# A fused transformer kernel on one core: x and mem also loaded turned, the small vectors as one array, and the first loads in another order

## The chip, the cores and the metric

The kernel runs on one core of a Trainium2 chip. The metric is the device time of one execution in microseconds (us); lower is better. A profiled execution is recorded separately; its trace gives the rows below, in us from the first instruction.

## The reference

Two transformer blocks stand one behind the other on x of 256 tokens by 1024 channels; mem holds another 256 rows of 1024. All is float32. The part that matters here is the first layer of the first block:

```
mem_n = rmsnorm(mem, norm_mem)
h = rmsnorm(x, norm_mix[0])
mkv = mem_n @ w_mem_kv[0]                  # 1024 x 512: keys and values of the memory
q, k, v, qm = split(h @ w_in_a[0])         # 1024 x 1536
y = concat(windowed_gqa(q, k, v, sink_a), memory_attn(qm, mk, mv))
x = x + y @ w_out[0]
x = x + (silu(gate) * up) @ w_down[0]      # h = rmsnorm(x, norm_ffn[0]); gate, up = h @ w_gate_up[0]
```

The second layer, with neighbourhood attention, and the second block (sparse attention, a recurrence, a convolved feed-forward layer) follow. rmsnorm divides each token by the root of its mean square and multiplies each channel by a gain. The kernel applies the gain per channel before the product and the root per token after it.

## The kernel before, in words

Every product is cut into parts. A part is a piece of a weight matrix of up to 1 MB (4 times 128 rows by 512 columns) that SP loads into one of four buffers raw0 to raw3. ACT rounds it to a high half (hi, the line with `split` in the ACT program) and DVE subtracts to get a low half (lo); there are three buffers of each. PE then makes three matmuls per 128 rows and per half of the tokens: high by high, low by high, high by low. The activations need the same two halves with the channels in the partitions: memTh, memTl for mem, xTh, xTl for x. SP may load into a raw buffer again as soon as the low half of the piece four before is made (`lo_made`). Parts 0 to 3 are the first product with mem (pieces of 0.26, 0.26, 0.52 and 1.05 MB), parts 4 and 5 the first tile of h @ w_in_a, parts 6 and 7 the second.

A class `Order` writes one list of steps; each engine's program goes through that list and emits what is its own in each step, so the list sets the order on ACT, DVE, POOL and PE alike. Steps that can wait go into a queue `later`, from which some are taken between parts and between the two chunks of twelve matmuls of a 1 MB part.

At the start SP loads mem (with the tokens in the partitions), four weight pieces, the small vectors in sixteen small loads, x, and then the weights. ACT's queue loads the identity and norm_mem, POOL's the constants of the scores. PE turns mem in four steps `memx` of two blocks of 128 channels each (four 128 by 128 transposes by the identity), x in four steps `xin`, and the vectors in one step `rows`; ACT writes the high and DVE the low half from the PSUM bank, each scaled with the gain of the channel. Step `memsq` squares and sums mem on ACT, DVE makes the mean, POOL the root; steps `sq` do the same for x, a half of the channels each.

When the mem tile is done, its evacuation stores one half in `mstage` on ACT and one on DVE, and in step `mk` PE turns mstage; mstage lies in the tensor `early`. Both the evacuation and `mk` need the root of mem. Lines: the transposes 833 and 835, the matmuls 855 to 857, the squares 1040, the evacuation 1087 and 1092, the high halves of weights 1175, of mem 1183 and of x 1195, the low halves 1600, 1624 and 1640, the root 1814, SP's loads from 1956 on.

Of the kernel before, what the change touches and what calls it, by code (L numbers as in the profile page):

```python
# [131 lines left out]
class Order:  # L132
# [53 lines left out]
    def put(self, *task):  # L186
        kind = task[0]
        if kind in ("memgain", "rows", "rel", "columns"):
            self.turn(task, ON_D)
            self.made.add(kind)  # L190
        elif kind == "memx":
            self.turn(task, ON_D)
# [4 lines left out]
        elif kind == "xin":  # L197
            self.turn(task, ON_D)
# [357 lines left out]
def build(nc, a, out):  # L556
    ctx = ExitStack()
    with ctx:
# [11 lines left out]
        d_mem, d_norm, d_x, d_rows, d_ident, d_const = (sem(n) for n in ("d_mem", "d_norm", "d_x", "d_rows", "d_ident", "d_const"))  # L570
# [42 lines left out]
        cols = sb("cols", [128, 128 + 96 + 88])  # L613
        small = sb("small", [128, 184])
# [15 lines left out]
        sink = small[:, 16:28]  # L630
        steep = small[:, 10:16]
# [4 lines left out]
        memgain = small[:, 144:152]  # L636
        m8 = small[:, 160:176]
# [16 lines left out]
        rows = early[:, 2048:2432].rearrange("p (n d) -> p n d", n=3)  # L654
        memx = early[:, 0:2048].rearrange("p (t d) -> p t d", t=2)
        memrow = early[0:8, 2432:2560]
# [36 lines left out]
        rel = small[0:32, 152:160]  # L693
# [55 lines left out]
        def ready(source, k):  # L749

            if source == "mem":
                return emptied(("memx", k // 2 * 2))
# [6 lines left out]
            what, l = source  # L759
            if what == "in":  # L760
                return emptied(("xin", l, k // 2 * 2))
# [62 lines left out]
        def tensor_program(e):  # L824
# [91 lines left out]
            for step in order.steps:  # L916
# [3 lines left out]
                elif kind == "memgain":  # L920
                    e.wait_ge(d_norm, 16)
                    e.wait_ge(d_ident, 16)
                    e.transpose(claim(step)[:, 0:8], memrow, ident[0:8, 0:8]).then_inc(x_full, 1)
                elif kind == "memx":
                    e.wait_ge(d_mem, 16)
                    turned(claim(step), blocks_of(memx, name[0] * 128, 2))
                elif kind == "rows":
                    e.wait_ge(d_rows, 256)
                    bank = claim(step)
                    e.transpose(bank[:, 0:128], rows[0:128, 0, :], ident)  # L930
                    e.transpose(bank[:, 128:224], rows[0:96, 1, :], ident[0:96, 0:96])
                    e.transpose(bank[:, 224:312], rows[0:88, 2, :], ident[0:88, 0:88]).then_inc(x_full, 1)
                elif kind == "xin":
                    s, k = name
                    if s == 0:
                        e.wait_ge(d_x, 16)
                    else:
                        e.wait_ge(acc_dve, order.res_at[s, k // 4])
                    turned(claim(step), blocks_of(xres, k * 128, 2))
                elif kind == "mk":  # L940
                    t_ = order.tile_of["mem", name[0], 0]
# [92 lines left out]
        def scalar_program(e):  # L1034
# [8 lines left out]
            def attention(stage, i):  # L1043
# [15 lines left out]
                if 0 <= i - 1 < n:  # L1059
# [6 lines left out]
                    else:  # L1066
                        e.wait_ge(max_made, 4 * stage + i)
                        src = x_bank(("S", stage, i - 1))[:, :].rearrange("p (t k) -> p t k", t=2)
                        if i - 1 >= len(s_slots[stage]):
                            e.wait_ge(x_full, filled(("P", stage, i - 1 - len(s_slots[stage]))))  # L1070
                        elif stage == 0:
                            e.wait_ge(x_full, filled(("memx", 6)))
# [94 lines left out]
            for step in order.steps:  # L1167
# [10 lines left out]
                elif kind == "memx":  # L1178
                    k = name[0]
                    e.wait_ge(x_full, filled(step))  # L1180
                    e.wait_ge(*emptied(("memgain",)))
                    for j in range(2):
                        e.activation(memTh[:, k + j, :], x_bank(step)[:, j * 256:(j + 1) * 256], ACT.Copy, scale=memgain[:, k + j:k + j + 1]).then_inc(x_high, 1)
                elif kind == "memsq":
                    e.wait_ge(d_mem, 16)
                    for j in range(2):
                        for t in range(2):
                            square(0, j, t, memx[:, t, j * 512:(j + 1) * 512])
                elif kind == "xin":
                    s, k = name  # L1190
                    gain = col((0, 2, 1, 3)[s])
                    e.wait_ge(x_full, filled(step))
                    e.wait_ge(*emptied(("rows",)))
                    for j in range(2):
                        e.activation(xTh[:, k + j, :], x_bank(step)[:, j * 256:(j + 1) * 256], ACT.Copy, scale=gain[:, k + j:k + j + 1]).then_inc(x_high, 1)
# [14 lines left out]
                elif kind == "pair":  # L1210
# [3 lines left out]
                    if l == 0 and what == "q" and at < 6:  # L1214
                        e.wait_ge(d_const, 32)
# [141 lines left out]
        def vector_program(e):  # L1357
# [50 lines left out]
            def soften(stage, i):  # L1408
# [10 lines left out]
                else:  # L1419
                    if i >= len(s_slots[stage]):  # L1420
                        e.wait_ge(x_full, filled(("P", stage, i - len(s_slots[stage]))))
                    if stage == 0:
                        e.wait_ge(d_const, 32)
# [170 lines left out]
            for step in order.steps:  # L1594
# [20 lines left out]
                elif kind == "memgain":  # L1615
                    e.wait_ge(x_full, filled(step))
                    e.tensor_copy(memgain, x_bank(step)[:, 0:8]).then_inc(x_dve, 1)
                elif kind == "memx":
                    k = name[0]
                    if k == 0:  # L1620
                        e.wait_ge(*emptied(("memgain",)))
                    e.wait_ge(x_high, order.high_at[step])
                    for j in range(2):
                        done = e.scalar_tensor_tensor(out=memTl[:, k + j, :], in0=x_bank(step)[:, j * 256:(j + 1) * 256], scalar=memgain[:, k + j:k + j + 1],
                                                      in1=memTh[:, k + j, :].bitcast(F), op0=ALU.mult, op1=ALU.subtract)
                    done.then_inc(x_dve, 1)
# [434 lines left out]
```

## Time and profile before

| what | us |
|---|---|
| median of 3 runs | 1112.36 |
| lowest and highest run | 1109.60, 1112.61 |
| the profiled execution | 1111.92 |
| its span, first to last instruction | 1110.1 |
| PE busy | 1041.9 (94%) |
| DVE busy | 738.4 (67%) |
| ACT busy | 587.1 (53%) |
| POOL busy | 116.8 (11%) |

The profiled execution's own time is 1.8 us longer than its span. The mean granted clock of PE is 0.975 of full speed. Busy shares are means over the whole span.

### The profile page before, as it was taken

The page shows a single profiled execution, that of the slowest core. Times are in us where ns is not written, and L with a number is a line of the kernel's source. Part 1 is how long each engine was busy: PE and PEld are TensorE (multiplying, and loading weights), DVE is VectorE, ACT ScalarE, POOL GpSimd, SP SyncE. Part 2 cuts the span into 40 slices and gives each one's busy share as a digit, 9 for nine tenths or more (in the row PEclk, how much of TensorE's full clock was granted, in tenths as well). Part 3 has the DMA queues.
Part 4 walks back from the last instruction along what each step waited for, and adds up shares of the span by engine and source line. Part 5 has one row for each costly group of instructions (what it writes and reads, how often), then busy time and mean ns, then how long its engine had stood idle before and what let it go on. Part 6 is the DMA issues. An engine that isn't in the chain of part 4 may idle for free.

```text
span 1110.1 us, 13563 instructions
## 1 busy us (share of the span) xinstructions
PE 1041.9 (94%) x5224; PEld 864.3 (78%) x5224; DVE 738.4 (67%) x984; ACT 587.1 (53%) x834; POOL 116.8 (11%) x159
## 2 busy tenths in 40 slices
PE   5997996999999999899999999998989989999996
PEld 5876875888888777788888888787767778888885
DVE  4667773465455567578888656669867766777753
ACT  6547562444345557544443445467656456666631
POOL 1013130000000013110000011012551000000001
PEclk9998998999999999999999979999999989999999
DMA  9655378655556441379999784435463535465441
GB/s 335 227 141 71 113 206 211 203 195 182 176 172 208 152 153 39 114 258 366 335 337 328 296 264 151 159 121 172 160 199 114 190 133 190 154 193 184 157 147 38
DMA packets 97825, 209.28 MB, mean 189 GB/s; under 512 B 5650, under 2 KB 13282, under 8 KB 94626
## 3 DMA queue, kind: packets, MB, share of 16 engines
q1 hardware_dynamic: 93313, 194.46, 52.0%
q0 software_dynamic: 4288, 13.89, 5.6%
q8 instruction: 42, 0.69, 0.3%
q14 instruction: 22, 0.17, 0.0%
q10 hardware_dynamic: 160, 0.07, 0.0%
HBM read 205.25 MB, written 4.57 MB: 189 GB/s over the span
## 4 chain that ended last, share of the span: by engine, by line
PE 73%; DVE 9%; ACT 7%; issue 4%; DMA 4%; POOL 2%; SPq 1%; ACTq 0%; DVEq 0%; POOLq 0%
PE bank L855 21%; PE bank L857 21%; PE bank L856 21%; PE bank L833 4%; ACT hi L1175 3%; DVE lo L1600 3%; DMA big<-scratch_rpb 2%; PE bank L869 2%; PE bank L835 1%; POOL big L1885 1%; PE bank L969 1%; DMA raw<-in_w_down 1%; DVE xres L1475 1%; DMA small<-in_sink_a 1%; DMA scratch_rpb<-in_rpb_b 1%
## 5 line engine op out<-in xcount | busy, mean ns | idle before, releaser
L1600 DVE TENSOR_TENSOR lo<-raw,hi 128x2048 fp32r<-128x2048 f32 (+1 forms) x164 | 367.4, 2242 | 219.1 <-ACT hi L1175 218.4
L1175 ACT ACTIVATE hi<-raw 128x2048 fp32r<-128x2048 f32 (+1 forms) x164 | 303.5, 1852 | 203.7 <-PE bank L857 156.9
L855 PE MATMUL bank<-hi,xTh 128*128 128x512 f32 (+2 forms) x896 | 346.9, 387 | 10.4 <-DVE lo L1600 10.4
L857 PE MATMUL bank<-hi,xTl 128*128 128x512 f32 (+2 forms) x896 | 337.7, 377 | 0.0
L856 PE MATMUL bank<-lo,xTh 128*128 128x512 f32 (+2 forms) x896 | 337.6, 377 | 0.0
L855 PEld LDWEIGHTS bank<-hi,xTh 128*128 128x128 f32 x896 | 170.3, 190 | 42.2 <-DVE lo L1600 11.0
L857 PEld LDWEIGHTS bank<-hi,xTl 128*128 128x128 f32 x896 | 170.0, 190 | 31.7
L856 PEld LDWEIGHTS bank<-lo,xTh 128*128 128x128 f32 x896 | 170.6, 190 | 28.6 <-issue 0.2
L855 PE MATMUL bank<-hi,hTh 128*128 128x512 f32 x264 | 103.5, 392 | 0.5 <-DVE lo L1600 0.5
L857 PE MATMUL bank<-hi,hTl 128*128 128x512 f32 x264 | 102.8, 389 | 0.0
L856 PE MATMUL bank<-lo,hTh 128*128 128x512 f32 x264 | 102.8, 389 | 0.0
L1814 POOL TENSOR_TENSOR rms<-rms,small 128x2 f32<-128x2 f32 x9 | 6.4, 715 | 510.3 <-DVE rms L1368 326.6
L855 PEld LDWEIGHTS bank<-hi,hTh 128*128 128x128 f32 x264 | 49.6, 188 | 11.0 <-DVE lo L1600 0.9
L857 PEld LDWEIGHTS bank<-hi,hTl 128*128 128x128 f32 x264 | 49.5, 188 | 10.4
L856 PEld LDWEIGHTS bank<-lo,hTh 128*128 128x128 f32 x264 | 49.6, 188 | 10.0
L1612 DVE SCALAR_TENSOR_TENSOR big<-raw,small,big 128x2048 f32<-128x2048 f32 x24 | 56.3, 2345 | 0.0
L1590 DVE SCALAR_TENSOR_TENSOR big<-bank,cols,big 128x255 f32<-128x255 f32 (+2 forms) x100 | 41.2, 475 | 8.7 <-ACT big L1339 7.7
L833 PE MATMUL bank<-const,nrm 128*128 128x128 f32 x201 | 35.8, 290 | 6.1 <-DVE nrm L1702 5.3
L1040 ACT ACTIVATE junk<-xres 128x512 bf16<-128x512 f32 x32 | 20.2, 632 | 37.0 <-DVE xres L1533 27.3
L833 PEld LDWEIGHTS bank<-const,nrm 128*128 128x128 f32 x201 | 27.6, 151 | 13.4 <-DVE nrm L1702 5.8
L1160 ACT ACTIVATE hTh<-bank 128x512 fp32r<-128x512 f32 x22 | 13.2, 598 | 33.1 <-PE bank L835 33.0
L1339 ACT ACTIVATE big<-bank,cols 128x256 f32<-128x256 f32 x44 | 22.4, 559 | 13.9 <-PE bank L835 13.9
(348 smaller groups left out, 1358.5 us busy)
## 6 DMA issues: line engine op xcount, KB each, us to landing
raw<-in_w_gate_up SPq DMA_DIRECT2D x44, 1024.0 KB, 5.4
raw<-in_w_down SPq DMA_DIRECT2D x30, 1024.0 KB, 5.1
raw<-in_w_ada SPq DMA_DIRECT2D x24, 1024.0 KB, 6.4
raw<-in_w_up SPq DMA_DIRECT2D x22, 1024.0 KB, 5.1
raw<-in_w_in SPq DMA_DIRECT2D x21, 1024.0 KB, 5.1
raw<-in_w_out SPq DMA_DIRECT2D x12, 1024.0 KB, 5.0
raw<-in_w_in_b SPq DMA_DIRECT2D x10, 1024.0 KB, 5.1
raw<-in_w_in_a SPq DMA_DIRECT2D x6, 1024.0 KB, 10.0
```

What stands on the lines that cost most here:

```text
L833: e.transpose(bank[:, i * 128:(i + 1) * 128], x, ident)
L855: e.matmul(o, sh, h[:, k, :], start=p.first and k == 0, stop=False)
L856: e.matmul(o, sh, lo[:, k, :], start=False, stop=False)
L857: done = e.matmul(o, sl, h[:, k, :], start=False, stop=p.last and k == p.nk - 1)
L869: done = e.matmul(bank[:, n * 256:(n + 1) * 256], q[x][:, n * 128:(n + 1) * 128], k[y], start=x + y == 0, stop=x == 1)
L1040: e.activation(junk[:, :], x, ACT.Square, accum_out=rms[i][:, 2 * j + t:2 * j + t + 1]).then_inc(squared, 1)
L1160: e.activation(o, view, ACT.Copy).then_inc(x_high, 1)
L1175: e.activation(hi_s[m % SPLITS][:, 0:n], raw[p.at % RAWS][:, 0:n], ACT.Copy).then_inc(hi_made, 1)
L1339: e.activation(cv[:, j, :], x_bank(task)[:, j * 256:(j + 1) * 256], ACT.Identity, bias=CVB(kt + j), scale=CVW(2, kt + j)).then_inc(conv_be ...
L1590: e.scalar_tensor_tensor(out=o[:, j, n:], in0=bank[:, j * 256:j * 256 + 256 - n], scalar=weights[j][n - 1], in1=o[:, j, n:], op0=ALU.mult, ...
L1600: e.tensor_tensor(lo_s[s][:, 0:n], raw[p.at % RAWS][:, 0:n], hi_s[s][:, 0:n].bitcast(F), ALU.subtract).then_inc(lo_made, 1)
L1612: e.scalar_tensor_tensor(out=piece, in0=raw[i % RAWS][:, :], scalar=small[:, k:k + 1], in1=piece, op0=ALU.mult, op1=ALU.add).then_inc(ada_ ...
```

## The change

x and mem are also given turned, with the channels in the partitions (`xT`, `memT`), and are loaded so into nrm and early. PE no longer turns them or the vectors, which arrive in one array of 128 by 330 on ACT's queue. mem in its first form goes into xres, for its squares alone; x comes into xres afterwards, on POOL's queue behind the root of mem, and the constants of the scores follow it there. The list has the steps of the start in another order.

```diff
         elif kind == "memx":
-            self.turn(task, ON_D)
             self.made |= {("mem", task[1]), ("mem", task[1] + 1)}
...
         elif kind == "xin":
-            self.turn(task, ON_D)
+            if task[1]:
+                self.turn(task, ON_D)
...
     def run(self):
-        self.put("memgain")
         for k in range(0, 8, 2):
+            self.put("memx", k)
             self.split_through(min(k // 2, SPLITS - 1))
-            self.put("memx", k)
-        self.later.append(("memsq",))
-        self.later.append(("rows",))
-        self.later.append(("relload",))
-        for j in range(2):
-            self.pieces(0, j)
+        self.later.extend([("rows",), ("xin", 0, 0), ("xin", 0, 2), ("memsq",), ("xin", 0, 4), ("xin", 0, 6), ("relload",), ("sq", 0, 0), ("sq", 0, 1)])
...
-        memx = early[:, 0:2048].rearrange("p (t d) -> p t d", t=2)
+        memT = early[:, 0:2048].rearrange("p (k t) -> p k t", k=8)
+        xT = nrm[:, :, :].rearrange("p t (k n) -> p (t k) n", k=4)
...
+            e.dma_start(cols[:, :], a["vectors"]).then_inc(d_vec, 16)
             e.dma_start(ident, a["constants"][:, 0:128]).then_inc(d_ident, 16)
-            e.dma_start(memrow, a["norm_mem"].rearrange("(k p) -> k p", p=128)).then_inc(d_norm, 16)
...
                 elif kind == "memx":
                     k = name[0]
-                    e.wait_ge(x_full, filled(step))
-                    e.wait_ge(*emptied(("memgain",)))
+                    if k == 0:
+                        e.wait_ge(d_vec, 16)
+                    e.wait_ge(d_memT[min(k // 2, 2)], 16)
...
                 elif kind == "memsq":
                     e.wait_ge(d_mem, 16)
                     for j in range(2):
                         for t in range(2):
-                            square(0, j, t, memx[:, t, j * 512:(j + 1) * 512])
+                            square(0, j, t, xres[:, t, j * 512:(j + 1) * 512])
...
-            e.dma_start(const[:, 128:1408], a["constants"][:, 128:1408]).then_inc(d_const, 16)
-            e.dma_start(steep, a["constants"][:, 1408:1414]).then_inc(d_const, 16)
...
                 if kind == "memsq":
                     e.wait_ge(pool_const, 2)
                     root(0, 1)
+                    e.dma_start(xres[:, :, :], a["x"][0].rearrange("(t p) d -> p t d", p=128)).then_inc(d_x, 16)
+                    e.dma_start(const[:, 128:1408], a["constants"][:, 128:1408]).then_inc(d_const, 16)
...
-            e.dma_start(memx, a["mem"][0].rearrange("(t p) d -> p t d", p=128)).then_inc(d_mem, 16)
-            for i in range(RAWS):
-                load(i)
...
+            e.dma_start(memT[:, 0:2, :], a["memT"][:, 0:2, :]).then_inc(d_memT[0], 16)
+            next_load(0)
+            next_load(1)
+            e.dma_start(memT[:, 2:4, :], a["memT"][:, 2:4, :]).then_inc(d_memT[1], 16)
+            next_load(2)
+            e.dma_start(memT[:, 4:8, :], a["memT"][:, 4:8, :]).then_inc(d_memT[2], 16)
+            next_load(3)
+            e.dma_start(xT[:, 0:4, :], a["xT"][:, 0:4, :]).then_inc(d_xT[0], 16)
+            next_load(4)
+            e.dma_start(xres[:, :, :], a["mem"][0].rearrange("(t p) d -> p t d", p=128)).then_inc(d_mem, 16)
+            e.dma_start(xT[:, 4:8, :], a["xT"][:, 4:8, :]).then_inc(d_xT[1], 16)
+            for i in range(5, len(plan)):
+                next_load(i)
```

`next_load` is the load of one weight piece with its wait for the low half of the piece four before.

The orders at the three places of which the prediction speaks, as the two programs have them. First ACT from its first step on; before, up to the second raw0 (memTh and xTh are high halves of mem and x, junk the discarded output of a square):

```order
L1175 ACT_TABLE_LOAD
L1175 ACTIVATE hi<-raw 128x512 [waits d_raw0]
...
L1040 ACTIVATE junk,rms<-early 128x512 [waits d_mem]
L1040 ACTIVATE junk,rms<-early 128x512 [waits squared] x3
L1175 ACTIVATE hi<-raw 128x2048 [waits part_done,d_raw3]
L1195 ACTIVATE xTh<-bank,cols 128x256 [waits x_dve,x_full]
L1195 ACTIVATE xTh<-bank,cols 128x256
L1175 ACTIVATE hi<-raw 128x2048 [waits part_done,d_raw0]
```

With the change, down to the evacuation of the mem tile (the last row):

```order
L1165 ACT_TABLE_LOAD [waits d_memT0]
L1165 ACTIVATE memTh<-early,cols 128x256 [waits d_vec]
...
L1180 ACTIVATE xTh<-nrm,cols 128x256 [waits d_xT0]
L1180 ACTIVATE xTh<-nrm,cols 128x256
L1156 ACTIVATE hi<-raw 128x2048 [waits part_done,d_raw3]
...
L1021 ACTIVATE junk,rms<-xres 128x512 [waits d_mem]
L1021 ACTIVATE junk,rms<-xres 128x512 [waits squared] x3
L1156 ACTIVATE hi<-raw 128x2048 [waits part_done,d_raw0]
...
L1021 ACTIVATE junk,rms<-xres 128x512 [waits squared,d_x]
L1021 ACTIVATE junk,rms<-xres 128x512 [waits squared]
L1068 ACTIVATE early<-bank,rms 128x256 [waits acc_first,root_made]
```

The table load has taken over a wait; two blocks of x have moved ahead of the high half of raw3, and the squares of mem from before that half to before the one of the second raw0. The squares of x stood ahead of the evacuation before too; the load for which they wait has moved. POOL with the change, from its memsets to the load of x:

```order
L1819 MEMSET ones 128x128
L1791 ISA
L1791 TENSOR_TENSOR rms<-rms,small 128x2 [waits mean_made,pool_const]
L1825 DMA xres<-in_x 128x2x1024
L1826 DMA const<-in_constants 128x1280
```

Before, the constants were POOL's first load, and x was loaded by SP ahead of w_in_a. PE with the change, at the end of the first chunk of part 4 (the rows on early are the turn of mstage, step `mk`):

```order
L851 MATMUL bank<-hi,xTh 128x512 [waits in_low]
L852 MATMUL bank<-lo,xTh 128x512
L853 MATMUL bank<-hi,xTl 128x512
L829 MATMUL bank<-const,early 128x128 [waits acc_dve,acc_act,d_ident]
L829 MATMUL bank<-const,early 128x128 x2
L831 MATMUL bank<-const,early 128x128
```

This turn has not moved; it stood between the same two chunks before. Beyond part 5 all five orders are the same but for bank numbers and one wait less here and there.

## Rows read from the trace of the kernel before

**Rows 1.** The page: busy times and the chain that ended last.

```profile
PE 1041.9 (94%) x5224; PEld 864.3 (78%) x5224; DVE 738.4 (67%) x984; ACT 587.1 (53%) x834; POOL 116.8 (11%) x159
...
PE 73%; DVE 9%; ACT 7%; issue 4%; DMA 4%; POOL 2%; SPq 1%; ACTq 0%; DVEq 0%; POOLq 0%
```

**Rows 2.** Waits of PE, 0 to 30: us in total, times, longest.

```profile
PE bank L930 <- DMA small<-in_sink_a: 4.0, 1, 4.0
PE bank L855 <- DVE memTl L1624: 1.2, 1, 1.2
```

**Rows 3.** The chain that ended last, 0 to 120: start, us, what.

```profile
9.15 7.19 DMA small<-in_sink_a
...
22.87 0.33 PE bank L833 x3
...
94.54 0.48 DVE early L1432
```

**Rows 4.** Windows: PE, PEld, DVE, ACT, POOL busy, PEclk, DMA share, GB/s.

```profile
1.00:2.00 1.00, 0.00 (x0) 0.00 (x0) 0.00 (x0) 0.17 (x1) 0.76 (x2) 1.00 0.16 8
2.00:3.00 1.00, 0.00 (x0) 0.00 (x0) 0.00 (x0) 1.00 (x1) 0.79 (x3) 1.00 0.58 131
...
10.00:11.00 1.00, 0.25 (x1) 0.28 (x2) 1.00 (x3) 1.00 (x4) 0.00 (x0) 1.00 1.04 383
...
13.00:14.00 1.00, 0.00 (x0) 0.00 (x0) 1.00 (x4) 0.97 (x4) 0.00 (x0) 1.00 1.19 192
...
16.00:17.00 1.00, 0.61 (x4) 0.61 (x4) 0.33 (x2) 1.00 (x3) 0.31 (x1) 0.50 1.03 399
```

**Rows 5.** Timeline of PE: start, us, engine, line, what.

```profile
17.46 0.63 PE L856 MATMUL bank<-lo,memTh 128*128 128x512 f32 x1
17.89 0.63 PE L857 MATMUL bank<-hi,memTl 128*128 128x512 f32 x1
...
29.55 0.39 PE L855 MATMUL bank<-hi,xTh 128*128 128x512 f32 x1
...
32.28 0.49 PE L833 MATMUL bank<-const,early 128*128 128x128 f32 x3
```

**Rows 6.** Timeline of ACT: its table load.

```profile
1.83 1.28 ACT L1175 ACT_TABLE_LOAD   x1 [1.83 <-issue]
```

**Rows 7.** Timelines of ACT, DVE and POOL: squares, halves, root, evacuation.

```profile
13.11 0.68 ACT L1040 ACTIVATE junk<-early 128x512 bf16<-128x512 f32 x1
...
16.04 1.89 ACT L1175 ACTIVATE hi<-raw 128x2048 fp32r<-128x2048 f32 x1
...
17.47 0.57 POOL L1875 DMA_DIRECT2D small<-in_rel_bias  x1
...
17.97 2.29 DVE L1600 TENSOR_TENSOR lo<-raw,hi 128x2048 fp32r<-128x2048 f32 x1 [0.20 <-ACT hi L1175]
...
20.15 0.84 ACT L1195 ACTIVATE xTh<-bank,cols 128x256 fp32r<-128x256 f32 x2 [2.21 <-PE bank L835]
...
24.07 0.63 ACT L1040 ACTIVATE junk<-xres 128x512 bf16<-128x512 f32 x1
...
25.45 1.90 ACT L1175 ACTIVATE hi<-raw 128x2048 fp32r<-128x2048 f32 x1
...
28.68 0.49 ACT L1087 ACTIVATE early<-bank,rms 128x256 f32<-128x256 f32 x1
```

**Rows 8.** DMA issues: KB each, us from issue to landing.

```profile
early<-in_mem SPq DMA_DIRECT2D x1, 1024.0 KB, 5.4
const<-in_constants POOLq DMA_DIRECT2D x1, 640.0 KB, 7.2
small<-in_rel_bias POOLq DMA_DIRECT2D x1, 1.0 KB, 5.3
gbc<-in_norm_final POOLq DMA_DIRECT2D x1, 512.0 KB, 7.9
```

**Rows 9.** Queues in windows 6:7 (two), 21:22, 479:480: packets, MB, share.

```profile
q0 software_dynamic: 61, 0.31, 74.7%
q1 hardware_dynamic: 60, 0.12, 30.6%
...
q0 software_dynamic: 35, 0.02, 7.5%
...
q0 software_dynamic: 45, 0.18, 44.6%
```

More of the change, by code:

```diff
@@ L187, in put @@
         kind = task[0]
-        if kind in ("memgain", "rows", "rel", "columns"):
+        if kind in ("rel", "columns"):
             self.turn(task, ON_D)
@@ L629, in build @@
         half_ = small[:, 8:10]
-        sink = small[:, 16:28]
-        steep = small[:, 10:16]
+        sink, steep = cols[:, 312:324], cols[:, 324:330]
         negsink = small[:, 80:92]
@@ L759, in ready @@
             what, l = source
+            if what == "in" and l == 0:
+                return in_low, k // 2 + 1
             if what == "in":
@@ L919, in tensor_program @@
                     matmuls(parts[name[0]], name[1])
[L920 to L933, printed above, removed]
+                elif kind == "xin" and name[0]:
                     s, k = name
[L935 to L938, printed above, removed]
+                    e.wait_ge(acc_dve, order.res_at[s, k // 4])
                     turned(claim(step), blocks_of(xres, k * 128, 2))
                 elif kind == "mk":
+                    e.wait_ge(d_ident, 16)
                     t_ = order.tile_of["mem", name[0], 0]
@@ L1973, in sync_program, with next_load @@
-            e.dma_start(sink, bass.AP(a["sink_a"].tensor, 0, [[0, 128], [1, 12]])).then_inc(d_rows, 16)
-            e.dma_start(xres[:, :, :], a["x"][0].rearrange("(t p) d -> p t d", p=128)).then_inc(d_x, 16)
             weight_no = {i: m for m, i in enumerate(order.weights)}
-            for i in range(RAWS, len(plan)):
-                if plan[i - RAWS][0] == "ada":
+            def next_load(i):
+                if i >= RAWS and plan[i - RAWS][0] == "ada":
                     e.wait_ge(ada_done, order.ada_at[i - RAWS])
-                else:
+                elif i >= RAWS:
@@ L2015, in shape_constants @@
     key = np.arange(256)
[L2016 removed]
+    c = np.zeros((128, 1408), np.float32)
     c[:, 0:128] = np.eye(128)
@@ L2028, in shape_constants, with vectors_of, turned_blocks @@
     return c
+def vectors_of(a):
+    rows = [a[n].reshape(-1, 128) for n in ("norm_mix", "norm_ffn", "norm_mem", "g_mix_2", "g_ffn_2", "c_2", "conv_rnn_w_2", "conv_rnn_b_2",
+                                            "b_rg_2", "b_ig_2", "lru_lambda_2")]
+    taps = a["conv_ffn_w_2"].reshape(-1, 128)
+    rows += [taps[0:88], a["b_in_2"][0, 2376:3400].reshape(-1, 128), taps[88:132], a["conv_ffn_b_2"].reshape(-1, 128)]
+    steep = [[0.125 * 2.0 ** (8.0 * (2 * k + (i >= 64) + 1) / 12) for k in range(6)] for i in range(128)]
+    sink = np.broadcast_to(a["sink_a"].reshape(1, 12), (128, 12))
+    return np.ascontiguousarray(np.concatenate([np.concatenate(rows).T, sink, steep], axis=1).astype(np.float32))
+def turned_blocks(x):
+    return np.ascontiguousarray(x[0].T.reshape(8, 128, 256).transpose(1, 0, 2))
 def distance_buckets():
@@ L2050 @@
     given["constants"] = shape_constants()
+    given["vectors"] = vectors_of(given)
+    given["xT"], given["memT"] = turned_blocks(given["x"]), turned_blocks(given["mem"])
     given["onehot"] = distance_buckets()
+    for name in ("norm_mix", "norm_ffn", "norm_mem", "g_mix_2", "g_ffn_2", "c_2", "conv_rnn_w_2", "conv_rnn_b_2", "b_rg_2", "b_ig_2", "lru_lambda_2",
+                 "conv_ffn_w_2", "conv_ffn_b_2", "sink_a"):
+        del given[name]
     for name, v in given.items():
```

71 lines of the change are left out of this document (24 added, 47 removed).

## The prediction

> **What bounds the kernel now.** I read the page first. TensorE (PE) is busy for 94% of the span and the chain that ended last lies on it for 73% [rows 1]; a DMA holds 4% of that chain. So time is won or lost only where PE stands idle or runs at the low clock, and this change touches only the first 40 us. Next I read PE's waits in that stretch: after its first matmuls it stands for 4.0 us until the sink vector lands [rows 2]. The chain explains it: sixteen small loads are issued by SP one by one behind the first four weight pieces, and the last of them, issued at 9.15, lands at 16.34 [rows 3]. From 16.39 to 35.5 PE never waits. The windows show that the transfers are saturated all that time: about 383 to 399 GB/s, with a dip to 192 while the small loads run [rows 4]. PE's clock is 0.50 after the wait: matmuls start 0.43 us apart at 17.46 and 17.89, where later twelve of them take 2.73 us, 0.23 each [rows 4, 5]. The mark I measure against is PE at 29.55, when it starts part 4 (the first piece of w_in_a), and at 32.28, when after twelve matmuls it turns mstage, the stored half of the mem tile [rows 5].
>
> **The change: bytes and landings.** The vectors come as one array; x and mem are loaded twice, once turned, so 2.1 MB are added to a saturated stretch. SP's order is now memT 0.26, raw0 0.26, raw1 0.26, memT 0.26, raw2 0.52, memT 0.52, raw3 1.05, xT 0.52, raw0 again 1.05, mem 1.05, xT 0.52, raw1 again 1.05 (MB), with 0.24 MB on ACT's queue. By 3.0 us 0.14 MB had moved, and then 0.395 MB per us [rows 4]. This gives xT's first half at 12.5, the second raw0 at 15.2, **mem at 17.9**, xT's second half at 19.2, the second raw1 at 21.8. The same sum for raw3 before comes out some 0.7 us too early, which I keep as its error. SP waits for the first low half before the second raw0; that is made by about 8 us while the queue still has work until 12.5, so this costs nothing.
>
> **PE's starts.** Eight turns of four transposes and the turn of the vectors leave PE. One such turn holds PE for 0.33 us [rows 3], so with the vectors' about 2 us of PE work after 16.39 go; they count only if PE is then the last to be ready. It isn't. ACT's table load of 1.28 us [rows 6] now stands behind the landing of the first memT piece, so the first high half begins near 5.5; parts 0 to 2 then run between about 8 and 15, hidden from the end. Part 3 needs raw3's high and low halves. ACT waits for xT at 12.5, converts two blocks (0.84), then 1.9 for the high half and 2.25 until the low half is usable [rows 7]: part 3 starts near 17.5 and ends at 23.0 warm, 24.4 with cold matmuls, before the next thing is ready in either case. Part 4's split stands in ACT's order behind the four squares of mem, now read from xres, and those wait for mem: 17.9, plus 2.93 for the squares, 1.9 and 2.3 for the two halves, gives 25.1 against 29.55. Up to here the change is **4.4 us ahead**.
>
> **The new wait.** The load of x has moved from SP at 9.56 to POOL, behind the root of mem's mean, because it overwrites mem in xres. From the first square to the issue behind the root it is 4.36 us before (13.11 to 17.47) [rows 7]; so x is issued at 22.3. In ACT's order two squares of x stand ahead of the evacuation of the mem tile; PE's turn of mstage waits for that evacuation and stands between the twelve and twelve matmuls of part 4, so all of PE is queued behind it. PE wants the turn at 25.1 + 2.73 = 27.8. It gets it at the landing of x, plus 1.38 for two squares (24.07 to 25.45), 0.5 for the evacuation [rows 7], 0.05 to be seen: landing + 1.95.
>
> When does x land? No row shows a 1 MB load on POOL's queue in a saturated stretch. Below: mem itself, 1 MB on SP's queue with constants beside it, took 5.4 us [rows 8], which gives 27.7. Above: norm_final took 7.9 us for 512 KB on POOL's queue [rows 8], twice that gives 38; but its 128 readers want one and the same row. Nearer is the 640 KB of constants on the same queue beside SP's weights. It is POOL's first load, issued by 2 us, and lands at 8.4; from 6 to 7 it moved 61 packets to SP's 60, and 0.31 of 0.43 MB, since its packets are 5 KB and SP's 2 KB [rows 9]. rel_bias, 1 KB, issued at 17.47 in full traffic, took 5.3 us, and its queue first shows packets after 21 [rows 8, 9]. So I take 4.0 us until x begins, then packet for packet 4 KB of x to 2 KB of weights, two thirds of 0.395, 3.9 us, and 0.1: **x lands at 30.3**. The bounds kept for the range are 27.7 and, at norm_final's 0.18 MB per us [rows 9] behind 4.5 us, 33.2. The Trainium skill (DMA: Bandwidth & Descriptors, section on queues, rings and completion order) says that each DMA engine goes round the queues packet by packet; by that rule the trace agrees where it counts 61 to 60. The section on the anatomy of one DMA fits a transfer from GpSimd as 2.0 us plus bytes by 436 GB/s; for x that is an estimate of 4.4 us in place of 8.0. The constants' 7.2 us for 640 KB speaks against it here.
>
> PE then goes on at 30.3 + 1.95 = 32.25, against 32.28 before: the 4.4 us are gone. It has stood for 4.4 us. Before, 4.0 us of idleness were followed by three windows at clock 0.50, 1.2 GHz [rows 2, 4]; seven matmuls at 0.43 in place of 0.23 are 1.4 us.
>
> **Everything behind it.** Part 5 needs raw1's low half at 29.0, and part 6, whose split stands behind the evacuation, is ready some 5 us after the turn and wanted 8.6 after it. The constants for the scores now follow x and land near 33, first used at 94.54 [rows 3]. The later order of all engines is the same but for bank numbers, and PE fills that stretch, so the shift is carried to the end. **Sum: 32.25 - 32.28 + 1.4 = +1.4 us** on the profiled execution's 1111.92, so 1113.3; the median of the runs stands 0.44 above that execution, so I say 1113.7, within 0.3% (3.3 us), about what a measurement here can tell from no change.
>
> **Rivals.** In general the shift is landing of x - 28.9 us if PE cools down, and 1.4 less if it doesn't.
> *x crawls (slower).* If x moves at norm_final's rate behind a start as late as that of rel_bias, it lands at 33 or later, PE stands from 27.8 to 35, and the shift is +4.3: 1116.7; decisive from a landing after 32.2. For it: norm_final's row. Against it: that load reads one row 128 times, and the constants, of the same kind as x, took over half. Chance 0.25.
> *x is quick.* If x takes mem's 5.4 us, it lands at 27.7, PE stands 1.8 us and stays warm (the 1.2 us of idleness before 10.75 [rows 2] left the clock at 1.00), shift -2.6: 1109.8. Against it: POOL's late start [rows 9]. Chance 0.14.
> *Hardly a wait (faster).* Faster by 0.3% needs PE to go on by 28.9 and warm, so x by 27.0. With mem's 5.4 us and mem itself 0.7 us early, the error I keep for landings, x is there at 27.0, PE stands 1.2 us, and the shift is -3.3; a start sooner than the constants' would give more. Against it: rel_bias and the constants both began late on this queue [rows 9]. The fit of the Trainium skill named above (DMA: Bandwidth & Descriptors) would put x at 26.7 and make this the likeliest case. Chance 0.09.
> My forecast, x between 29.2 and 32, has 0.52.
>
> **Numbers.** Faster than 1109.0 needs the last rival or a part of the third: 0.1. Slower than 1115.7 is the first rival: 0.25. The rest, 0.65, is within 0.3%. The range leaves out the last rival and the worst of the first: from a landing at 28 without cooling (-2.3) to one at 33 with it and half a us of later mem (+4): 1110.2 to 1116.9, widened by the scatter of the median to 1110.0 and 1117.3.
>
> **What would show it.** In the changed trace: no wait of PE for the sink; part 4's first matmul (with xTh) near 25; one new wait of PE of 4 to 5 us ahead of the transposes of early, ended by ACT's evacuation; the first square of x on ACT idle until x lands near 30; x 8 us from issue to landing; POOL's queue silent for some 4 us after 22.3; clock 0.50 after the wait. It is wrong if mem lands far from 18, if x lands before 28 or after 32, or if a wait beyond 40 us differs from before by more than the shift.

## The result, and the profile after

| | before | after |
|---|---|---|
| median of 4 runs, us | 1111.45 | 1119.88 |
| lowest and highest, us | 1109.60, 1112.61 | 1118.68, 1121.13 |
| the profiled execution, us | 1111.92 | 1121.13 |
| its span, us | 1110.1 | 1119.3 |
| mean granted clock | 0.975 | 0.975 |

The ratio is 1.0078, with an interval of 1.0058 to 1.0099: the change makes the kernel about 8.4 us slower, where I had forecast +1.4 and a range up to 1117.3. One execution of a later run, `allgap`, ran at a granted clock of 0.746 and took 1312.73 us; it is left out of every figure. The page of the changed kernel, busy times and chain (before: [rows 1]):

```profile
PE 1045.8 (93%) x5188; PEld 859.4 (77%) x5188; DVE 738.4 (66%) x982; ACT 587.8 (53%) x834; POOL 115.8 (10%) x159
...
PE 70%; DVE 10%; ACT 7%; DMA 6%; issue 4%; POOL 2%; DVEq 0%; ACTq 0%; SPq 0%; POOLq 0%
```

PE has 36 fewer operations and yet is busy for 3.9 us more. That is the first hint that something outside the first 40 us has changed. The start first. Waits of PE from 0 to 40 (before: [rows 2]), and of the chain that ended last the pieces behind them (start, us, what):

```profile
PE bank L851 <- DVE lo L1584: 11.2, 2, 8.4
PE bank L829 <- ACT early L1068: 4.1, 1, 4.1
```

```profile
8.80 10.46 DMA xres<-in_mem
19.28 0.73 ACT junk L1021 x2
...
22.81 0.64 POOL rms L1791
23.45 8.12 DMA xres<-in_x
31.59 0.73 ACT junk L1021 x2
32.57 0.31 issue
33.06 0.37 ACT early L1068
33.52 0.88 PE bank L829 x3
34.61 0.43 PE bank L851
```

The wait for the sink is gone, and the new one is there as it was described: mem, its four squares, the root, x, two squares, the evacuation, PE's turn. ACT's timeline has the same with the steps between:

```profile
4.63 1.28 ACT L1165 ACT_TABLE_LOAD   x1 [4.63 <-DMA early<-in_memT]
...
14.00 0.91 ACT L1180 ACTIVATE xTh<-nrm,cols 128x256 fp32r<-128x256 f32 x2 [1.32 <-DMA nrm<-in_xT]
14.82 1.90 ACT L1156 ACTIVATE hi<-raw 128x2048 fp32r<-128x2048 f32 x1
...
19.28 0.63 ACT L1021 ACTIVATE junk<-xres 128x512 bf16<-128x512 f32 x1 [1.76 <-DMA xres<-in_mem]
...
22.17 1.90 ACT L1156 ACTIVATE hi<-raw 128x2048 fp32r<-128x2048 f32 x1
...
31.59 0.63 ACT L1021 ACTIVATE junk<-xres 128x512 bf16<-128x512 f32 x1 [4.11 <-DMA xres<-in_x]
```

And windows behind the wait (columns as in [rows 4]): PE stands from 29.5 to 33.5 and then runs at a granted clock of 0.50 for some 3 us (up to 36.5 its 512-column matmuls start 0.43 us apart, behind that 0.23).

```profile
29.00:31.00 2.00, 0.45 (x3) 0.03 (x1) 1.57 (x2) 0.00 (x0) 0.00 (x0) 1.00 1.03 406
31.00:33.00 2.00, 0.00 (x0) 0.00 (x0) 0.00 (x0) 1.38 (x5) 0.00 (x0) 1.00 1.05 393
33.00:35.00 2.00, 1.48 (x6) 1.41 (x7) 0.88 (x2) 2.00 (x5) 0.00 (x0) 0.59 1.03 329
35.00:37.00 2.00, 2.00 (x7) 1.57 (x6) 1.02 (x1) 1.97 (x4) 0.00 (x0) 0.56 1.05 387
```

To see how the start carries on, I laid ACT's 164 splits of weights of the two traces side by side, in order. The one that begins at 35.76 before begins at 38.5 after: +2.8 us, and so it stays up to 77 us. But then the distance grows, to 8.7 us at the last split: by 0.16 us in every part of a down product, where the operand is hT (5.60 us for 24 matmuls instead of 5.44), and there are 33 such parts. (Stretches at a clock of 0.50, 58 us in all before and 57 after, fall in other places in each execution and move the distance by up to 2 us either way.) The lines by form show it as well. TensorE on hT, the kernel before, then after (the last two numbers ahead of the second bar: us busy, mean ns of one):

```profile
L855 PE MATMUL bank<-hi,xTh 128*128 128x512 f32 x768 | 309.1, 402 | 10.4 <-DVE lo L1600 10.4
...
L855 PE MATMUL bank<-hi,hTh 128*128 128x512 f32 x264 | 103.5, 392 | 0.5 <-DVE lo L1600 0.5
L857 PE MATMUL bank<-hi,hTl 128*128 128x512 f32 x264 | 102.8, 389 | 0.0
```

```profile
L851 PE MATMUL bank<-hi,xTh 128*128 128x512 f32 x768 | 310.5, 404 | 10.7 <-DVE lo L1584 10.7
...
L851 PE MATMUL bank<-hi,hTh 128*128 128x512 f32 x264 | 104.9, 397 | 0.0
L853 PE MATMUL bank<-hi,hTl 128*128 128x512 f32 x264 | 104.2, 395 | 0.0
```

Ends of matmuls are modelled, so starts say it better. PE in the same stage, before and after: 21 products from 296.18 to 300.94 are 0.227 us each, 24 from 295.64 to 301.24 are 0.233.

```profile
296.18 0.39 PE L855 MATMUL bank<-hi,hTh 128*128 128x512 f32 x1
296.41 0.39 PE L856 MATMUL bank<-lo,hTh 128*128 128x512 f32 x1
...
300.94 0.39 PE L855 MATMUL bank<-hi,hTh 128*128 128x512 f32 x1
```

```profile
295.64 0.39 PE L851 MATMUL bank<-hi,hTh 128*128 128x512 f32 x1
295.87 0.40 PE L852 MATMUL bank<-lo,hTh 128*128 128x512 f32 x1
...
301.24 0.39 PE L851 MATMUL bank<-hi,hTh 128*128 128x512 f32 x1
```

From here on "ns per product" is the median from one start to the next of 512-column matmuls with the named operand. Before: 227 on all of them, a nanosecond more or less. After: 227 on xTh and xTl; 231 to 234 on hT, qy, q2y and on the pair keep and rTl (the high and the low half of one operand, used in the same triples).

What can tell hT from xTh? Two lines of the change that I had taken for bookkeeping, and that the diff above leaves out:

```diff
-        cols = sb("cols", [128, 128 + 96 + 88])
-        small = sb("small", [128, 184])
+        cols = sb("cols", [128, 312 + 12 + 6])
+        small = sb("small", [128, 152])
```

Tensors are laid one behind the other, each size rounded up to 32 bytes per partition. In the kernel before, all the large ones start at a multiple of 64 bytes. Here `cols` takes 96 bytes more and `small` 128 less, so everything declared behind them (early, qy, hT, rTl, q2y) starts 32 bytes lower, off such a multiple. The split weights hi and lo, xTh, xTl and keep are declared ahead of them and stay.

### The profile page after: what moved, and what is told of

Its sections match the earlier page's. It is cut to its first block, busy times and chain, and to the rows that moved or that the text cites. A ratio compares the mean times of both kernels' runs of the same rounds, so it can differ in the third digit from the quotient of the medians.

```text
span 1119.3 us, 13449 instructions
## 1 busy us (share of the span) xinstructions
PE 1045.8 (93%) x5188; PEld 859.4 (77%) x5188; DVE 738.4 (66%) x982; ACT 587.8 (53%) x834; POOL 115.8 (10%) x159
## 4 chain that ended last, share of the span: by engine, by line
PE 70%; DVE 10%; ACT 7%; DMA 6%; issue 4%; POOL 2%; DVEq 0%; ACTq 0%; SPq 0%; POOLq 0%
PE bank L851 21%; PE bank L853 20%; PE bank L852 20%; PE bank L829 3%; DVE lo L1584 3%; ACT hi L1156 3%; DMA big<-scratch_rpb 2%; PE bank L865 1%; DMA raw<-in_w_gate_up 1%; PE bank L831 1%; POOL big L1861 1%; DMA xres<-in_mem 1%; PE bank L950 1%; DMA xres<-in_x 1%; DMA scratch_rpb<-in_rpb_b 1%
## 5 line engine op out<-in xcount | busy, mean ns | idle before, releaser
L852 PEld LDWEIGHTS bank<-lo,xTh 128*128 128x128 f32 x896 | 171.2, 191 | 28.9 <-issue 0.2
L1021 ACT ACTIVATE junk<-xres 128x512 bf16<-128x512 f32 x36 | 22.8, 632 | 43.4 <-DVE xres L1517 27.7
```

The costliest lines, as they stand in the source:

```text
L852: e.matmul(o, sh, lo[:, k, :], start=False, stop=False)
L1021: e.activation(junk[:, :], x, ACT.Square, accum_out=rms[i][:, 2 * j + t:2 * j + t + 1]).then_inc(squared, 1)
```

## The experiments

Ratios are to the kernel before, whose median was 1110 to 1112 us each time it ran beside them; a thousandth is 1.1 us. The interval of a difference between two ratios is some 2 us either way, 3 us for the runs with few executions.

**One: give the old addresses back (`pad`).**

```diff
-        small = sb("small", [128, 152])
+        small = sb("small", [128, 160])
```

> The changed kernel with one edit: small is 160 floats wide where the change made it 152, so that every tensor declared behind it (early, mem's and q's pairs, hT, rTl and the rest) starts at the address it had before the change, a multiple of 64 bytes; in the changed kernel they start 32 bytes lower. Theory (the address of the stationary operand costs time in the matmul): from one matmul of 512 columns to the next the changed kernel took 234 ns where the operand is hT, qy, q2y or rTl, against 227 before, and 227 in both where it is xTh or xTl, which did not move. 792 + 192 + 48 + 192 such matmuls by 7 ns are 8 us; so 6 to 8 us faster than the changed kernel, 1112 to 1114 us, and 227 ns everywhere. Rival (something in the flow of the transfers or the clock, set going by the new start, slows the down products): the address plays no part, 1119 to 1121 us and 234 ns on hT as before this edit.

Measured: 1113.94 us, ratio 1.0022 (1.0007 to 1.0037), against 1.0078 (1.0058 to 1.0099) for the change as it was: the eight unused floats win 6 us. 227 ns per product on every long stage. TensorE on hT:

```profile
L851 PE MATMUL bank<-hi,hTh 128*128 128x512 f32 x264 | 103.5, 392 | 0.2 <-DVE lo L1584 0.2
```

**Two: take them from the kernel before (`shift`).**

```diff
-        small = sb("small", [128, 184])
+        small = sb("small", [128, 176])
```

> The kernel before the change with one edit: small is 176 floats wide instead of 184, so that every tensor behind it starts 32 bytes lower, as in the changed kernel; the start of the program stays as it was. Theory (address): 234 ns from matmul to matmul on hT, qy, q2y and rTl, 227 on xTh and xTl, and 6 to 8 us slower than before, about 1118 us. Rival (the new start does it): 1111 us and 227 ns everywhere.

Measured: 1120.82 us, ratio 1.0077 (1.0057 to 1.0097). The old start with the new addresses is as slow as the change. 227 ns on xT, 234 on hT, 233 to 234 on qy. So the start is not the cause of the slow products, and the addresses alone are.

```profile
L855 PE MATMUL bank<-hi,hTh 128*128 128x512 f32 x264 | 104.9, 397 | 0.1
```

**Three: which tensor (`gap`).**

```diff
-        small = sb("small", [128, 152])
+        small = sb("small", [128, 160])
...
         big = sb("big", [128, 6144])
+        gap = sb("gap", [128, 8])
```

> The changed kernel with small at 160 floats and a gap of 32 bytes behind big, so that of all tensors only those in the space behind big that is shared by hT, the pairs of stage 1, rTl and stage 2's tensors start off a multiple of 64 bytes; early, the statistics, junk, big and stage 0's pairs start on one. Theory (it is the operand of the matmul itself): hT, rTl, q2y and qy of stage 1 take 234 ns again and qy of stage 0 227, 5.5 to 8 us slower than without the gap. Rival (it is a small tensor that ACT, DVE or POOL write beside the matmuls, junk, statistics or big): no slower than without the gap, 227 ns everywhere.

Measured: 1118.21 us, ratio 1.0064 (1.0043 to 1.0085), 4.3 us more than `pad`, a little less than expected; hT at 234 ns, rTl and keep at 228 to 240, xT at 227. The query operand qy tells it best, within one kernel: that of the first layer lies ahead of the gap and takes 227 to 228 ns, that of the second lies behind it and takes 232 to 235. So it is the operands of the matmuls themselves, and not junk, the statistics, early or big. One row does not fit: keep lies ahead of the gap, on a multiple of 64 like the weights, and yet takes 232 and 240 (227 in `pad`); its partner rTl lies behind. This kernel's hT:

```profile
L852 PE MATMUL bank<-hi,hTh 128*128 128x512 f32 x264 | 105.0, 398 | 0.0
```

**Four: the other operand (`movgap`).** hT and all tensors behind small lie on multiples of 64 again, and the split weights and xT don't.

```diff
         raw = [sb(f"raw{i}", [128, 2048]) for i in range(RAWS)]
+        gap = sb("gap", [128, 8])
         hi_s = [sb(f"hi{i}", [128, 2048], R) for i in range(SPLITS)]
```

> The changed kernel with small as it has it (152 floats) and 32 bytes of gap ahead of the split weights, so that hi, lo, xres, nrm, xTh, xTl, constants, keep, cols start 32 bytes off a multiple of 64, and all behind small (hT, early and the rest) on one. Theory (it is the stationary operand whose address counts): products on xTh and xTl at 234 ns from one to the next, 2304 of them by 7 ns are 16 us, products on hT at 227; 14 to 18 us slower than with small at 160. Rival (either operand counts): hT at 234 too, some 20 us slower or more. Rival (only the tensors behind small matter, by where they lie against each other or the banks): about as with small at 160.

Measured: 1122.67 us, ratio 1.0097 (1.0074 to 1.0119). That is 8.3 us more than `pad` by the ratios, not 14 to 18, and my theory of the stationary operand falls: the products on xT, with both operands off, take 227 ns; those on hT, with hT itself on a multiple and only the weights off, take 234. The 792 + 192 + 48 + 192 products on hT, qy, q2y and keep with rTl by 7 ns are 8.6 us. So far the cost is not one operand's address but how the two lie to each other. On hT, and on xT, which takes what it took in the change (310.5, 404):

```profile
L852 PE MATMUL bank<-hi,hTh 128*128 128x512 f32 x264 | 104.9, 397 | 0.0
...
L852 PE MATMUL bank<-hi,xTh 128*128 128x512 f32 x768 | 311.2, 405 | 6.8 <-DVE lo L1585 6.8
```

**Five: all off alike (`allgap`, and again as `allgap2`).**

```diff
+        gap = sb("gap", [128, 8])
         hi_s = [sb(f"hi{i}", [128, 2048], R) for i in range(SPLITS)]
...
-        small = sb("small", [128, 152])
+        small = sb("small", [128, 144])
...
-        rel = small[0:32, 144:152]
+        rel = small[0:32, 16:24]
```

> The changed kernel with 32 bytes of gap ahead of the split weights, and small at 144 floats (rel_bias moves to columns of small that are used late), so that hi, lo, xTh, xTl, keep and all tensors behind small, hT among them, start 32 bytes off a multiple of 64 alike. The run with the gap alone took 227 ns a product on xTh, with both operands off, and 234 on hT, with the weights off and hT on. Theory (what costs is that the two operands lie differently to a multiple of 64 bytes, not that either is off one): 227 ns on every operand, hT included, and the time of the kernel with small at 160, 1112 to 1116 us. Rival (a moving operand that is off costs 7 ns on some operands but not on xTh for a reason of its own): 234 on hT, 1119 to 1123 us.

> The same kernel as the run with all operands 32 bytes off alike, once more: the profiled execution of that run was one at a clock of 0.746 throughout, so that it shows no product at full clock. Theory (what costs is that the two operands lie differently to a multiple of 64 bytes): 227 ns a product on xTh and on hT alike, 1114 to 1118 us. Rival (a moving operand off a multiple costs on hT whatever hT's own address): 227 on xTh, 234 on hT.

Measured: 1116.83 (four executions) and 1118.06 us, ratios 1.0059 (1.0037 to 1.0081) and 1.0054 (1.0038 to 1.0071). Neither theory comes out whole. In the second run xT is at 227 ns, and on hT the three steps of a triple are at 232, 226 and 229: between the two levels. So on hT and qy a difference in how the operands lie is enough for 234 (the change and runs two to four), and being off alike is not enough for 227. The pair keep and rTl does not follow even that: in the change keep and the weights are both on multiples of 64, rTl alone is off, and keep's own products take 231 to 233. 227 everywhere is shown only where every operand is on a multiple of 64. What tells xT from hT when both are off I did not find. One lead, which no run tests: xTh begins 65536 bytes behind the first hi and hTh, in `allgap`, 128704; both are multiples of 64, but the second is none of 128 (in `pad` it is 128768, which is one).

**Six: take the wait for x away (`xfree`).** Base: `pad`. mem gets room of its own, where q's high half is written later; x needn't wait for mem's squares.

```diff
+        with ExitStack() as sc:
+            skip, memx = sb("skip", [128, 9728], F, sc), sb("memx", [128, 2, D], F, sc)
...
-            e.dma_start(xres[:, :, :], a["mem"][0].rearrange("(t p) d -> p t d", p=128)).then_inc(d_mem, 16)
+            e.dma_start(memx[:, :, :], a["mem"][0].rearrange("(t p) d -> p t d", p=128)).then_inc(d_mem, 16)
...
-                    e.dma_start(xres[:, :, :], a["x"][0].rearrange("(t p) d -> p t d", p=128)).then_inc(d_x, 16)
...
             for i in range(5, len(plan)):
                 next_load(i)
+                if i == 6:
+                    e.dma_start(xres[:, :, :], a["x"][0].rearrange("(t p) d -> p t d", p=128)).then_inc(d_x, 16)
```

> The changed kernel with small at 160 floats, and mem for the squares loaded into space of its own (over the place where q's high half is written later) instead of into x's place, and x issued by SP behind the seventh load of weights, with no wait for the squares. Theory (the wait for x at mem's first turn and the cold clock behind it are the lasting part of the start): PE ends part 4 at about 31.8 us and goes straight on, where it now goes on at 33.5 and then at half clock; 2.5 to 4 us faster than the kernel with small at 160 alone. Rival (mem's late landing alone sets the start; what the wait cost is caught up later by slack in the splits): less than 1 us faster. Rival (x, moved forward, takes its bandwidth from the weights): part 4 or the next two parts start over 1 us later than now, and it is no faster or slower.

Measured: 1110.34 us, ratio 0.9983 (0.9971 to 0.9996): 3.9 us less than `pad` by the ratios. In its profiled execution the later pieces of the turned mem, and mem itself, landed about a microsecond later than in `pad`, and x only at 30.2 behind the weights; still PE's wait shrank from 4.1 to 1.6 us, and the clock stayed at 1.00 behind it. I had expected the turn without a wait; the gain came all the same.

**Seven: leave the loads, change only the order (`sqlate`).** Base: `pad`.

```diff
-        self.later.extend([("rows",), ("xin", 0, 0), ("xin", 0, 2), ("memsq",), ("xin", 0, 4), ("xin", 0, 6), ("relload",), ("sq", 0, 0), ("sq", 0, 1)])
+        self.later.extend([("rows",), ("xin", 0, 0), ("xin", 0, 2), ("memsq",), ("xin", 0, 4), ("xin", 0, 6), ("relload",)])
         self.linear("mem", 0, 0, 512, len(FIRST), "mem", 2)
+        self.later.extend([("sq", 0, 0), ("sq", 0, 1)])
```

> The changed kernel with small at 160 floats, and x's squares of both halves put into the order behind mem's first turn instead of ahead of mem's evacuation, so that ACT no longer stands at x's landing when part 4 ends; loads, queues and buffers stay. Theory (the wait for x stands there by the order alone, and what it costs is the wait and the cold clock behind it): ACT evacuates mem's tile at about 31.8 us, mem's first turn is at about 32.2 instead of 33.5, the granted clock stays at 1.0 behind it, and the kernel is 2.5 to 4 us faster than with small at 160 alone, as the one with mem in space of its own was. Rival (ACT stands at x's landing at 31.6 anyway, one step later, and the next split and the roots of x are late by it): under 1 us faster, and PE waits at the first evacuation of v or k or for a split behind 36 us.

Measured: 1109.69 us, ratio 0.9989 (0.9977 to 1.0001), 3.7 us less than `pad`. ACT evacuates at 27.4 already, and PE turns mem at 30.7, after 1.2 us of waiting for DVE's half of the evacuation:

```profile
30.73 0.52 PE L830 MATMUL bank<-const,early 128*128 128x128 f32 x3 [1.24 <-DVE early L1434]
```

Windows of `pad`, then of `sqlate`:

```profile
31.00:33.00 2.00, 0.00 (x0) 0.00 (x0) 0.00 (x0) 1.37 (x5) 0.00 (x0) 1.00 1.03 380
33.00:35.00 2.00, 1.46 (x7) 1.34 (x8) 0.88 (x2) 2.00 (x5) 0.00 (x0) 0.80 1.05 346
35.00:37.00 2.00, 2.00 (x6) 1.52 (x6) 1.00 (x1) 1.97 (x4) 0.00 (x0) 0.50 1.05 388
```

```profile
31.00:33.00 2.00, 2.00 (x12) 1.70 (x11) 0.49 (x2) 2.00 (x3) 0.00 (x0) 1.00 1.03 384
33.00:35.00 2.00, 2.00 (x10) 1.64 (x10) 2.00 (x1) 1.88 (x6) 0.00 (x0) 1.00 1.03 329
35.00:37.00 2.00, 2.00 (x11) 1.65 (x10) 1.22 (x4) 1.97 (x5) 0.13 (x1) 1.00 1.05 386
```

With 1.2 us of idleness the clock stays at 1.00, with 4.1 it falls to 0.50. In between the length of the wait does not decide it: after 2.8 us ahead of 19.10 in the change the clock was 0.50 from 19.7 on, after 2.9 us ahead of 20.21 in `xfree` and 3.4 us ahead of 28.94 in `own2` (below) it stayed at 1.00. The wait for x stood on PE's path by ACT's order alone; here ACT comes to its squares at 33.3 and finds it there.

**Eight: mem's squares behind the split of part 4 too (`both`).** Base: `sqlate`. In the list `("memsq",)` goes behind `("xin", 0, 4)`, and mem's load behind that of the second half of xT.

> As the kernel with x's squares behind mem's first turn, and besides mem's rows are loaded behind the second half of the turned x, and mem's squares stand behind the split of part 4 instead of ahead of it. Theory (the other lasting part of the start is mem's landing at 19.3 us ahead of ACT's squares, which hold the split of part 4 from about 19 to 22.2 us): the split of part 4 begins when its weights land, 18.5 to 20 us, part 4 begins at 24.5 to 25.5 instead of 26.4, and it is 1 to 2 us faster than with x's squares moved alone. Rival (x is issued later, since POOL issues it behind mem's squares, and part 5 or the roots of x become late by what part 4 gains): within 0.7 us of that kernel.

Measured: 1109.72 us, ratio 0.9988 (0.9972 to 1.0005), the same as `sqlate`, and from 47 to 77 us the two traces stand alike, 1.5 us ahead of the kernel before. The part-4 split moved from 22.2 to 18.6 us and PE's turn from 30.7 to 28.9; then the rival took it back, x lands later, and its squares stand ahead of the next split:

```profile
33.65 0.63 ACT L1022 ACTIVATE junk<-xres 128x512 bf16<-128x512 f32 x1 [2.06 <-DMA xres<-in_x]
...
36.61 1.90 ACT L1157 ACTIVATE hi<-raw 128x2048 fp32r<-128x2048 f32 x1
```

**Nine: all three (`own`).** `both`, with mem's room and x's load of `xfree`, the latter at `i == 5`.

> The changed kernel with small at 160 floats, x's squares behind mem's first turn, mem's squares behind the split of part 4, mem in space of its own, and x issued by SP behind the sixth load of weights. Theory (the kernel with both moves had mem's turn 1.9 us earlier and lost it again at x, which landed at 33.6 us and held the split of part 7 to 36.6): x lands by 29 us, nothing waits for it, and it is 1 to 2.5 us faster than with x's squares moved alone, 1107 to 1109 us. Rival (the rate of all transfers is what holds the start, and x then pushes the weights of parts 6 and 7 behind their due time): within 0.7 us of that kernel, 1109 to 1110.5 us, and a split waits for raw weights between 24 and 36 us.

Measured: 1105.93 us, ratio 0.9969 (0.9952 to 0.9985): faster than both kernels, by 3.4 us than before and by some 12 than the change. x is there when ACT wants it:

```profile
31.64 0.63 ACT L1024 ACTIVATE junk<-xres 128x512 bf16<-128x512 f32 x1
...
34.60 1.90 ACT L1159 ACTIVATE hi<-raw 128x2048 fp32r<-128x2048 f32 x1
```

Its interval overlaps that of `sqlate`, so that it beats `sqlate` by 2 us is likely and not certain. The traces say the same: from 47 to 77 us it stands 3.2 us ahead of the kernel before, `sqlate` 1.5.

**Ten: and part 3's split ahead of x's cast (`own2`).** In the list a step without work stands behind `("rows",)`, so that `("xin", 0, 0)` comes one place later.

> As the kernel before it in this list, and the first casts of the turned x stand behind the split of part 3 instead of ahead of it, where ACT waited 1.3 us for the turned x's landing at 14.0 us and then cast it for 0.8 us. Theory (part 3 waits for this cast, not for its weights): the split of part 3 begins at 12.7 to 13.3 us instead of 14.8, part 3 at 17 to 17.6 instead of 19.1, and the kernel is a further 0.8 to 2 us faster. Rival (the weights of part 3 land at about 14.5 us themselves, or part 4's do not land before 19, so that the wait moves from part 3 to part 4): within 0.5 us of the kernel before it.

Measured: 1107.73 us, ratio 0.9974 (0.9957 to 0.9992), no gain. Part 3 did begin at 17.0 instead of 19.1, but mem's turn stayed where it was, 28.94 against 29.04. PE of `own`, then of `own2`:

```profile
19.08 0.50 PE L854 MATMUL bank<-hi,memTh 128*128 128x512 f32 x1 [2.36 <-DVE lo L1587]
29.04 0.52 PE L832 MATMUL bank<-const,early 128*128 128x128 f32 x3 [1.47 <-DVE early L1436]
```

```profile
17.01 0.50 PE L854 MATMUL bank<-hi,memTh 128*128 128x512 f32 x1 [0.34 <-DVE lo L1587]
28.94 0.52 PE L832 MATMUL bank<-const,early 128*128 128x128 f32 x3 [3.43 <-DVE early L1436]
```

All 2 us went into a wait for DVE's half of the evacuation. It stands behind the low half of part 5's weights (25.31, 2.29 us), whose high half ACT makes only after mem's squares, and mem lands at 20.5. The rival had the size, no gain, but neither of the two places it named is this one.

**Eleven: a smaller load on ACT's queue (`ident`).** Base: `pad`; the identity's load is issued behind mem's second casts instead of at the start.

> The changed kernel with small at 160 floats, and the load of the identity (64 KB in packets of 512 bytes) issued by ACT behind the second pair of mem's casts instead of at the start. Theory (the queue of ACT with its small packets takes turns from SP's queue in the first microseconds, which is why the transfers start slowly and mem landed at 19.3 us where 17.9 was predicted): the pieces of the turned mem land 0.3 to 1 us earlier and mem at 18.6 to 19.0 us; 0.3 to 1 us faster. Rival (the slow start is SP's own issue, one transfer per 0.45 us, and the packets of 2 KB of the turned pieces): mem at 19.2 to 19.4 as before, no faster.

Measured: 1114.70 us, ratio 1.0025 (1.0006 to 1.0044); mem's first square at 19.72 against 19.28. No gain, and mem did not land sooner, so the identity's small packets are not what slows the first transfers; those of the vectors, on the same queue, no run takes away.

## Why the prediction was wrong, by its steps

**The step that failed** is "Everything behind it": the later order of all engines is the same, so the shift is carried to the end. The order was the same; the addresses were not. It cost 6 us (`pad` against the change), in a stage that I did not look at since no instruction of it had changed. Worked from the traces, 33 parts of hT by 0.16 us are 5.3 us. No rival had it. With the addresses given back the change takes 1113.94 us, where I had said 1113.7. That they are so close is in part luck: by the ratio the start costs 2.4 us (0.8 to 4.1), where I had said 1.4.

The Trainium skill (SBUF — State Buffer, section "Who interferes with whom") gives PE two independent read ports, one for the moving operand and one for the weight load, and says that PE never waits on anyone. Runs one to five differ from that picture in one respect: a product takes 227 or 234 ns by where its two operands lie. The measurement decides; whether the two reads are what collides, no run here shows.

**The start, step by step.**
- The sink's wait goes, and with it 2 us of turns that don't count: right.
- Table load behind the first memT, first high half near 5.5: 5.93.
- xT's first half at 12.5, mem at 17.9: wrong by 1.5 and 1.4 us, 14.0 and 19.3. I had taken 0.395 MB per us from 3 us on. The windows 3:4, 5:6 and 6:7 of the changed kernel had 288, 342 and 270 GB/s, where before they had 394, 411 and 431:

```profile
3.00:4.00 1.00, 0.00 (x0) 0.00 (x0) 0.00 (x0) 0.00 (x0) 0.00 (x0) 1.00 0.83 288
...
5.00:6.00 1.00, 0.00 (x0) 0.00 (x0) 0.00 (x0) 0.99 (x2) 0.00 (x0) 1.00 1.04 342
6.00:7.00 1.00, 0.00 (x0) 0.00 (x0) 0.13 (x1) 1.00 (x3) 0.00 (x0) 1.00 0.94 270
```

  In the first 7 us 351 of its 959 packets are under 2 KB, before 179 of 635. That is where it differs; `ident` shows that the identity's 128 packets of 512 bytes don't explain it, and the rest is open.
- Part 4 at 25.1: 26.4, late by mem.
- x's 8.0 us from issue to landing: 8.1. POOL's queue was silent until after 27 (3.5 us and more behind the issue; I had 4.0). From 28 to 30 it moved 200 packets to SP's 15, which looks as if it didn't share. But there SP had little under way: its load of 19.07 landed at 29.14, and the next, issued at 26.42, shows its first packets at 30. From 30 to 32, with both at work, it is 128 to 125. In `both` SP's load was issued at 22.89, and from 29 to 31 the queues take turns packet for packet, as I had it:

```profile
q0 software_dynamic: 129, 0.53, 67.4%
q1 hardware_dynamic: 132, 0.27, 35.9%
```

- PE's turn at 32.25: 33.52. The cold clock at +1.4: between the turn (+1.2) and the split that follows (+2.8) another 1.5 went.

So the term of the start was +2.8 us in the trace for +1.4 predicted, and +2.4 by the ratio of `pad`; it was within the range, and the mis-sized part is mem's landing: 1.4 us late, it made x's issue 1.2 us and its landing 1.3 us late. `xfree` and `sqlate` confirm the mechanism: wait and clock together were worth 3.9 and 3.7 us by the ratios, and 3.0 and 4.4 us at 74 us in the traces.

That this shift is then carried to the end, no single trace shows. In `pad` it is +2.9 us at 74 us, +1.3 from 197 to 480 and nothing at the end. Its two large steps lie where the clock is at 0.50: from 183 to 195, and from 654 to 692, where the kernel before had 17 us of it and `pad` 10. The twelve executions of `pad` alone reach from 1111.2 to 1118.2 us, so only the medians tell.

Two figures of the prediction don't come out of its own rows, and nothing hangs on them: the upper landing is 22.3 + 4.5 + 1.05 / 0.18 = 32.6 and not 33.2, and 1116.9 belongs to a shift of 4.5 and not 4.

## What to carry to other kernels

When a change resizes any tensor, list the start addresses of everything behind it: here eight floats too few in a table of small vectors cost more than the whole rebuilt start. Keep both operands of the large matmuls on multiples of 64 bytes, and compare the time from start to start of matmuls in stages that the change leaves alone. And where a wait stands on PE's path, ask whether the data or only the place in an order puts it there; moving x's squares back in the order won what a buffer of its own for mem won.

## What the chip showed that I hadn't expected

- On hT a 512-column product took 227 ns from start to start with both operands on multiples of 64 bytes, 234 with one of them 32 bytes off, and 226 to 232 with both 32 bytes off; xT took 227 in either case, and was never off alone. keep took 231 to 233 with itself and the weights on multiples and its low half rTl off. Weight loads in themselves took the same (about 188 ns).
- Products of 256 columns didn't change: on v 115 ns before and 116 after. But there both operands had moved alike; no run has one of them off alone.
- The granted clock after a wait of PE: 1.00 after 1.2, 1.6, 2.9 (`xfree`) and 3.4 us (`own2`), 0.50 after 2.8 and 4.1 us (the change).
